# The gate of a gated linear attention as the exponential of minus ln(1 + exp(-g)), joined with the norm's root

## The reference

```python
S, o_a = gla_scan(q, k, v, loga)            # 4 heads, dk 64, dv 128
...
o_a = rmsnorm(o_a, onorm).reshape(B, T, GLA_V) * jax.nn.silu(g.astype(f32))
```

## Time and profile before

| | |
|---|---|
| median of 3 runs | 3760.03 us (3751.36 to 3761.77) |
| profiled execution | 3757.36 us |
| its span, first to last instruction | 3755.3 us |
| TensorE, VectorE, ScalarE, GpSimd busy | 93%, 41%, 30%, 16% |
| mean granted TensorE clock | 0.960 of full |
| stage `gla` | 438.3 us to 543.7 us of the span; next stage from 544.7 |
| `cumulate` (VectorE, 0.88 and 1.67) | 2.55 us |
| `queries` (two halves) | 1.80 us, once 2.73 |
| `norm` over a third, over a head | 1.67, 0.58 us |
| `bend` over a third, over a head | 1.62, 0.52 us |
| `masked`, add, multiply of the state | 0.29, 0.42, 0.42 us |
| pass of ScalarE over a third, over a head | 1.37 to 1.39, about 0.50 us |
| a head's total (TensorE) and Ln (ScalarE) | 0.64 us between chunks, 0.55 us |

### The profile page before, as it was taken

One profiled execution on the slowest core, in us unless ns is written; L12 is line 12 of the kernel. 1 busy time (PEld: TensorE's weight loads), 2 busy tenths in 40 slices (PEclk: granted clock), 3 DMA queues, 4 the chain that ended last, 5 costly groups with the idle time before them and its releaser, 6 DMA issues. The chain is left out here.

```text
span 3755.3 us, 61413 instructions
## 1 busy us (share of the span) xinstructions
PE 3493.1 (93%) x26430; PEld 3279.7 (87%) x26430; DVE 1554.2 (41%) x2533; ACT 1129.2 (30%) x2104; POOL 586.9 (16%) x705
## 2 busy tenths in 40 slices
PE   8899989999999999989899883776999999999998
PEld 8898769989999999985798783765998999999997
DVE  6345463443332322335246576446334332232233
ACT  6223263233211211226345422444223321121123
POOL 1000112002100100121221375320100210010012
PEclk9999989999999999997999996898999999999999
DMA  7422312102111111116547567864200111111111
GB/s 228 103 60 64 104 34 84 35 23 46 46 46 45 48 49 46 43 43 195 188 157 238 193 177 150 189 131 109 88 25 23 46 50 46 46 46 45 46 42 67
DMA packets 457388, 323.15 MB, mean 86 GB/s; under 512 B 105134, under 2 KB 435214, under 8 KB 453870
## 3 DMA queue, kind: packets, MB, share of 16 engines
q1 hardware_dynamic: 402874, 280.72, 26.3%
q10 hardware_dynamic: 43876, 18.99, 2.0%
q0 software_dynamic: 10368, 19.51, 1.6%
HBM read 232.29 MB, written 86.96 MB: 85 GB/s over the span
## 5 line engine op out<-in xcount | busy, mean ns | idle before, releaser
L83 PE MATMUL ps<-am_y,am_wh 128*128 128x352 f32 x4896 | 1178.0, 322 | 0.0
L83 PE MATMUL ps<-am_h,am_wh 128*128 128x352 f32 x3648 | 881.5, 325 | 1.2 <-DVE am_h L1398 1.2
L83 PEld LDWEIGHTS ps<-am_y,am_wh 128*128 128x128 f32 x4896 | 853.5, 188 | 1.3
L83 PE MATMUL ps<-am_y,am_wl 128*128 128x352 f32 x2448 | 789.7, 323 | 0.0
L83 PEld LDWEIGHTS ps<-am_h,am_wh 128*128 128x128 f32 x3648 | 634.0, 188 | 4.3 <-DVE am_h L1398 1.4
L83 PE MATMUL ps<-am_h,am_wl 128*128 128x352 f32 x1824 | 586.0, 321 | 0.0
L83 PEld LDWEIGHTS ps<-am_y,am_wl 128*128 128x128 f32 x2448 | 459.9, 188 | 0.0
L83 PEld LDWEIGHTS ps<-am_h,am_wl 128*128 128x128 f32 x1824 | 343.1, 188 | 0.0
L1485 POOL TENSOR_TENSOR am_silu<-am_silu,rs 128x352 f32<-128x352 f32 x132 | 126.5, 960 | 1234.3 <-ACT am_silu L1342 1234.3
L1074 DVE TENSOR_TENSOR x<-ps,x 128x352 f32<-128x352 f32 x240 | 125.7, 524 | 450.8 <-PE ps L83 441.6
L83 PE MATMUL ps<-rw_parts,rw_wh 128*128 128x352 f32 (+1 forms) x1152 | 289.2, 333 | 23.0 <-PEq L2513 13.1
(11 more groups left out here) (326 smaller groups left out, 4645.7 us busy)
## 6 DMA issues: line engine op xcount, KB each, us to landing
am_w<-in_ffn_w SPq DMA_DIRECT2D x120, 512.0 KB, 3.9
rw_ra_d<-tb_rk SPq DMA_DIRECT2D x8, 1056.0 KB, 8.2
rw_kbt_d<-tb_gk SPq DMA_DIRECT2D x8, 1056.0 KB, 4.0
rw_gg_d<-tb_gk SPq DMA_DIRECT2D x8, 1056.0 KB, 6.5
fr_w<-in_xa_wk SPq DMA_DIRECT2D x8, 1024.0 KB, 5.4
fr_w<-in_xa_wv SPq DMA_DIRECT2D x8, 1024.0 KB, 5.4
am_w<-in_xa_wq SPq DMA_DIRECT2D x16, 512.0 KB, 4.1
am_w<-in_xa_wo SPq DMA_DIRECT2D x16, 512.0 KB, 4.1
```

The costliest lines, as they stand in the source:

```text
L83: mm = nc.tensor.matmul(out, l, part, start=start and n == 0, stop=stop and n == 2)
```

## The change

The gate is no longer computed by Silu. ScalarE computes exp(-g) (`gate_exp`) and ln(1 + that) (`gate_log`) into a new buffer `soft_g`. VectorE adds half the logarithm of the mean square to it (`join`), and `scale`, now with scale -1, gives root and sigmoid in one: exp(-(0.5 ln(ms) + ln(1 + exp(-g)))). `bend` multiplies by g itself, which stays in its buffer. In the thirds 0 and 1 `join` is one instruction over the third; for the last third it is one per head. The table load by hand at L420 goes.

The order changes too. For the next third: soft from r = 1 to 2, cumulate from 3 to 4, grow from 5 to 6, queries from 6 to 7. For the last third: join at r = 5 (on VectorE), scale from 6 to 7; norm and bend stay at 8 and 9. gate_exp and gate_log stand at r = 8 and 9 of the gate's own third, on ScalarE, where silu stood at r = 7 of the next third (and at 9 for the last).

```diff
--- before.py
+++ after.py
@@ -105,7 +105,7 @@
         qp, kp, dec = sb("qp", NCH, 2, 2, C), sb("kp", NCH, 2, 2, C), sb("dec", 2, NCH)
         state, kv, g = sb("state", 4, 2, GLA_DV), sb("kv", 2, 2, P), sb("gm", 2, P)
         mask, keep, gain, eps, one = sb("mask", P), sb("keep", BLK), sb("gain", 1), sb("eps", 1), sb("one", 1)
-        sq, rsg = sb("sq", GLA_HEADS, BLK), sb("rs", GLA_HEADS, BLK)
+        sq, rsg, soft_g = sb("sq", GLA_HEADS, BLK), sb("rs", GLA_HEADS, BLK), sb("sg", GLA_HEADS, BLK)
         z_in, qk_in, v_in, g_in = ([sem(f"{s}_in{i}") for i in range(2)] for s in ("z", "qk", "v", "g"))
         mask_in, keep_in, gain_in, init_in, set_, cleared = (
             sem(s) for s in ("mask_in", "keep_in", "gain_in", "init_in", "set", "cleared"))
@@ -113,8 +113,8 @@
             sem(s) for s in ("act_step", "z_set", "cums", "grown", "dec_set", "qp_set", "kp_set", "vr_set"))
         turned, kv_out, made, g_out, s_done, s_added, state_ready, y_done, y_out = (
             sem(s) for s in ("turned", "kv_out", "made", "g_out", "s_done", "s_added", "state_ready", "y_done", "y_out"))
-        squares, sums, logs, scales, gated, normed, done, stored = (
-            sem(s) for s in ("squares", "sums", "logs", "scales", "gated", "normed", "done", "stored"))
+        squares, sums, logs, joined, scales, gated, normed, done, stored = (
+            sem(s) for s in ("squares", "sums", "logs", "joined", "scales", "gated", "normed", "done", "stored"))
         A, G, S, Y, TOTAL = 0, 2, 3, 5, 7
         block = ctx.enter_context(nc.Block())
         two = lambda d, r, b: d[r:r + 2 * P, columns(b)].rearrange("(a p) t -> p a t", p=P)
@@ -297,6 +297,13 @@
                 nc.vector.tensor_tensor(state[:, new(c)], state[:, new(c)], dec[:, :, c:c + 1].broadcast_to([P, 2, GLA_DV]),
                                         ALU.mult).then_inc(state_ready, 1)
 
+            def join(b, h0, h1):
+
+                dve.wait_ge(logs, GLA_HEADS * b + h1)
+                dve.wait_ge(gated, 2 * b + 2)
+                nc.vector.scalar_tensor_tensor(out=rsg[:, h0:h1], in0=rsg[:, h0:h1], scalar=0.5, in1=soft_g[:, h0:h1],
+                                               op0=ALU.mult, op1=ALU.add).then_inc(joined, 1)
+
             def norm(b, h0, h1):
                 at = y[:, h0:h1, columns(b)]
                 nc.vector.scalar_tensor_tensor(out=at, in0=at, scalar=gain[:, 0:1], in1=rsg[:, h0:h1], op0=ALU.mult,
@@ -317,10 +324,12 @@
                 add(c)
                 b, r = c // PB, c % PB
                 if b + 1 < BLOCKS:
-                    if r == 3:
+                    if r == 4:
                         cumulate(b + 1)
-                    if r == 6:
+                    if r == 7:
                         queries(b + 1)
+                if b and r == 5:
+                    join(b - 1, 0, GLA_HEADS)
                 if b and r == 8:
                     if b == 1:
                         dve.wait_ge(gain_in, 16)
@@ -328,11 +337,10 @@
                     norm(b - 1, 0, GLA_HEADS)
                 if b and r == 9:
                     dve.wait_ge(normed, b)
-                    dve.wait_ge(gated, b)
                     bend(b - 1, 0, GLA_HEADS).then_inc(done, 1)
             b = BLOCKS - 1
-            dve.wait_ge(gated, BLOCKS)
             for h in range(GLA_HEADS):
+                join(b, h, h + 1)
                 dve.wait_ge(scales, b + h + 1)
                 norm(b, h, h + 1)
                 dve.wait_ge(normed, b + h + 1)
@@ -387,12 +395,18 @@
                 nc.scalar.activation(rsg[:, h], ps[:, bank, 0:BLK], ACT.Ln, bias=eps[:], scale=1.0 / P).then_inc(logs, 1)
 
             def scale(b, h0, h1):
-                act.wait_ge(logs, GLA_HEADS * b + h1)
-                nc.scalar.activation(rsg[:, h0:h1], rsg[:, h0:h1], ACT.Exp, scale=-0.5).then_inc(scales, 1)
-
-            def silu(b):
+                act.wait_ge(joined, b + (h1 if b == BLOCKS - 1 else 1))
+                nc.scalar.activation(rsg[:, h0:h1], rsg[:, h0:h1], ACT.Exp, scale=-1.0).then_inc(scales, 1)
+
+            def gate_exp(b):
                 act.wait_ge(g_in[b % 2], 16 * (b // 2 + 1))
-                nc.scalar.activation(sg[:, b % 2], sg[:, b % 2], ACT.Silu).then_inc(gated, 1)
+                if b:
+                    act.wait_ge(joined, b)
+                nc.scalar.activation(soft_g[:], sg[:, b % 2], ACT.Exp, scale=-1.0).then_inc(gated, 1)
+
+            def gate_log(b):
+                act.wait_ge(gated, 2 * b + 1)
+                nc.scalar.activation(soft_g[:], soft_g[:], ACT.Ln, bias=one[:]).then_inc(gated, 1)
 
             soft(0)
             grow(0)
@@ -407,17 +421,16 @@
                 if b and 1 <= r <= GLA_HEADS:
                     log(b - 1, r - 1, TOTAL)
                 if b + 1 < BLOCKS:
-                    if r == 1:
+                    if r == 2:
                         soft(b + 1)
-                    if r == 5:
+                    if r == 6:
                         grow(b + 1)
-                if b and r == 6:
+                if b and r == 7:
                     scale(b - 1, 0, GLA_HEADS)
-                if b and r == 7:
-                    silu(b - 1)
-                if b == BLOCKS - 1 and r == 9:
-                    silu(b)
-                    nc.scalar.preload_act_table_set(LN_EXP)
+                if r == 8:
+                    gate_exp(b)
+                if r == 9:
+                    gate_log(b)
             b = BLOCKS - 1
             square(b, 0, 1)
             square(b, 1, 2)
```

## The result

The changed kernel takes 3769.82 us (median of 7 runs, 3765.65 to 3770.62) against 3754.02 for the kernel before (7 runs, 3748.53 to 3761.77): a ratio of 1.0037, 95% interval 1.0027 to 1.0046. It is slower by 0.4%, a little more than the 0.3% that I had called the bound of measurement, and the whole interval lies above 1. The profiled execution of the changed kernel took 3769.74 us, its span is 3767.6; against the 3755.3 of before that is 12.3 more. The medians are 15.8 apart; nearly all of the other 3.5 us is that the execution profiled before, 3757.36, lay 3.3 above the median of its kernel.

The account below looks back on a forecast made before the run. The stage was taken as a recurrence over 33 chunks between barriers, whose gains or losses go straight into the time. 1.05 + 3.1 − 2.5 + 3.3 = 4.95 on the profiled 3757.36 gave 3762.3 us, range 3751 to 3772.

Parts of the forecast that it names:

- The case that I gave 0.88: Whole kernel: the time stays the same as before, within 0.3% (11.3 us).
- the slower case: Whole kernel: slower by more than 0.3%, through lasting half clock or table loads that stay; chance 0.07.
- Loads and Silu gone: ScalarE in the stage: five table loads vanish, Exp and Ln passes cost 0.02 to 0.1 us each.
- rival 2: Stage: ScalarE was the bound, VectorE's passes hide, four stalls go; 3752, or 3747.4 if the clock holds; chance 0.14.
- Block 0: Before chunk 11: GpSimd's key products of the next third come late for TensorE; +1.05 us, bounds 0 and 1.7.
- rival 1: Chunks 15 to 24: the clock holds there, that term is −0.2 and the end 0.8 shorter; 3758.2; chance 0.18.
- Block 1: Chunks 15 to 24: queries wait for GpSimd, VectorE is crowded, the clock falls; +3.1 us, bounds −0.2 and +4.8.
- the second wait: Chunks 15 to 24: GpSimd's second key product also delays queries, ending at 12.4 instead of 10.8; bound +4.8.
- Block 2: Chunks 24 to 30: 12.4 us against 14.91 before; −2.5 us, bounds −2.9 and −1.5.
- The end: Chunk 30 to the last product: heads in turn, 2.39 us each, none overlapping; +3.3 us, bounds +1.5 and +5.
- the third: From chunks 18 to 22 on: the clock stays at half, 1.37 us per chunk; 3771.3 to 3773; chance 0.05.

Follow-up runs that it names:

- e1: The changed kernel with soft, cumulate, grow and queries back in their old chunks; 3764.36 us, 1.0023 to the kernel before.
- e3: The kernel before with Exp (scale -1) in place of Silu and no load, so only the five loads go; 3752.27 us, 1.0002.
- e4: The changed kernel with one unread TensorE product ahead of make(10) and one ahead of make(11); 3760.91 us, 1.0017 to the kernel before.
- e2: The kernel before, Silu kept, with soft, cumulate, grow and queries placed as changed, scale and silu one chunk later; 3763.93 us, 1.0025.
- e6: The changed kernel with GpSimd's key products of the last third held until VectorE's queries are done; 3770.41 us, 1.0045 to the kernel before.
- e5: e4 with three more unread TensorE products ahead of the scores in make(21); 3755.36 us, 0.9997 to the kernel before.
- e8: e1 without join in the thirds 0 and 1, whose gate then lacks the sigmoid; 3756.45 us, 0.9999 to the kernel before.
- e9: e1 with e7's overlapped end and join cut into one-head pieces behind chunks 13 to 16 and 24 to 27; 3758.91 us, 1.0014.
- e7: The changed kernel, end overlapped: all four squares first, next head's join between norm and product; 3769.15 us, 1.0033 to the kernel before.
- e10: e9 with one unread TensorE product each in make(21) and make(22); 3751.28 us, 0.9995 to the kernel before.
- e11: The kernel before with one unread TensorE product each in make(21) and make(22) and ahead of scan(30) and scan(31); 3752.54 us, 0.9998.
- e12: e10 with e6's wait of GpSimd's key products for the queries in the last third; 3751.30 us, 0.9992 to the kernel before.

## Why the prediction was right or wrong

The time lies in the range (3751 to 3772), 7.5 us above the 3762.3 forecast. The case that I gave 0.88, within 0.3%, is not the one that the ratio of 1.0037 names, though its interval reaches down to 1.0027; the slower case had 0.07. Between profiled executions the sum was +4.95, and 12.4 came. That the time is in the range is in part luck: I counted from an execution of 3757.36, and the seven runs put the kernel before at 3754.02. Counted as a difference the range ended at +14.6, and the medians are 15.8 apart.

*Loads and Silu gone* was right in kind: no load behind the first until 556. That its two passes are nearly free rests on e1, where both stand in block 0 and the pitches there are within 0.12 us of before. In size the reading of the stalls erred in block 1. The 1.48 us behind out(18) and the 1.07 behind out(23) were read as the loads', and e3 shows that without any load block 1 takes as long as before: 0.9 of the first stays, and the second load stood beside TensorE at half clock, as the fifth did. The sum didn't use these two prices; rival 2 did.

*Block 0* is the step that failed: "**+1.05 us** (bounds 0 ... and 1.7, a chunk)". The wait was found, in its place and nearly in its size (0.93 us of idle), and its own price was right: 1.00 us, as e4 shows. But I priced it at its own length alone. TensorE then ran at half clock for 17 us, up to chunk 14, so that the two stretches cost 7.9 us instead of 1.05. The order alone does that (e2), putting it back undoes it (e1), and filling the idle undoes it with everything else in place (e4). I had written the fall of the clock into block 1 and into the rivals, and for block 0 said nothing of it. The rows for a guess were at hand: 498 to 503, with 3.76 busy of 5.00, stands ahead of the fall in the earlier trace rows, and 475 to 480 of the changed kernel has 3.60 of 5.00, idle in three pieces of which the wait is the last and longest. The row that I cited for rival 1, 1.57 busy of 2.50 at full clock, speaks the other way. Why the clock held there and fell here isn't shown; that it holds when the pause is filled is.

*Block 1* came out at its upper bound: forecast +3.1, bound +4.8 "with the second wait too", measured +4.83. I took only the queries to wait, and for GpSimd's first product alone. The state's product ahead of them waited for the first (1.84 us) and the queries for the second (3.28; e6 shows that they need 1.80 without it), and GpSimd had begun 0.6 us earlier than I had it, because its decay copy, when it comes first, takes 0.22 and not 0.94. The fall came where it was forecast. That the figure meets the bound is in part chance: at out(21) the changed kernel was 0.8 us behind the sum, and the other 0.9 came in the pitch from out(23) to out(24), 3.92, where the sum had a plain 3.05 although that chunk holds a head's total, which is slower at half clock too. e5's 23.25 at full clock is near the sum's 23.3, with out(20) 1.0 later than in the sum and the rest made up behind it. That join and not the gate's passes is the cause is shown by e8, in the order of e1.

The Trainium skill, "SBUF — State Buffer", section Terms, says that VectorE and GpSimd lock their shared ports for a whole instruction. The traces agree: the queries take 1.80 us without GpSimd's products beside them (e6), 3.20 (e9) and 3.28 (the changed kernel) with them, and GpSimd, which holds the ports first, takes 3.49 for both products in the changed kernel, as it does behind the queries in e6.

*Block 2* was right, −2.60 against −2.5.

*The end* was right in kind, +2.02 against +3.3: heads in turn, at 2.14 and not 2.39, for join took 0.53 and not 0.58 and the changes of engine came out shorter. The first Ln came 6.7 us behind out(30), not 7.0. e7 shows the chain.

Of the rivals, the third had the right mechanism, more time at half clock, and the wrong place; the second, that VectorE's passes hide, is refuted by e8.

## What to carry to other kernels

A pause of TensorE isn't priced by its own length where a granted clock hangs on how busy the engine is: 0.93 us of waiting cost 7.9 here, 1.0 for itself and 6.9 by the clock. Look how much the stretch around it idles already, and price the fall as well. Work moved by one step meets other work: write down for each moved pass what shares its port or its engine in the new place, and which of two engines gets there first, for 0.05 us decided about 1.4. And an idle-filling product of TensorE is the quickest test of whether it is the clock: if it brings the time back while adding work, it is.

## What was not expected of the hardware

The same kind of fall has different lengths: about 10 us at half clock in the kernel before and in e2, about 17 us both times in the changed kernel, about 24 in e1, about 3 in e10, with TensorE without a pause in the records for nearly all of it. What sets the length is open.

A GpSimd copy of 128x22 took 0.22 us when it came first and 0.94 to 0.95 when VectorE's queries did; the record of an instruction includes its wait for the other engine, so a duration read beside another engine's work is not the instruction's own.

The part of the kernel outside the stage, with the same code, took 3639.8 us in one profiled execution (e11) and 3655.3 in another (e7). Most of it lies in one stretch, from the table load at 1827 to the one at 2587 us of the kernel before (760.0 us there): it takes 752.8 in e11 and 765.3 in e7. Why is open. This spread kept gains of 4 to 5 us in the stage (e11, e12) from being shown in the time.
